# Where a decoder block's side work stands: the first operand sums on VectorE, and the weight combinations two at a time

## The reference

```
proj = rms_norm(x) @ w_in                      # pool, gate, conv a, conv b, gate, q, k, v, gate
y_pool = window means of u minus u, mapped per group, scaled
y_conv = silu(layer_norm(depthwise_conv31(a * sigmoid(b)) + bias)) @ conv_pw
y_attn = softmax(q k^T + alibi, window 128, sinks) @ v       # 8 query heads, 2 key heads
y      = concat(y_pool * silu(g1), y_conv * silu(g2), y_attn * silu(g3))
out    = rms_norm(x + y @ w_out) * final_g
```

## Time and profile before

| | |
|---|---|
| median of three runs | 1467.82 us (1467.74 to 1469.67) |
| profiled execution | 1469.99 us, its span 1468.3 us |
| busy | PE 97%, DVE 77%, ACT 34%, POOL 28% |
| attention stage | to about 660 us |
| output stage | from about 1140 us |

### The profile page before, as it was taken

One profiled execution on the slowest core, in us unless ns is written; L12 is line 12 of the kernel. 1 busy time (PEld: TensorE's weight loads), 2 busy tenths in 40 slices (PEclk: granted clock), 3 DMA queues, 4 the chain that ended last, 5 costly groups with the idle time before them and its releaser, 6 DMA issues.

```text
span 1468.3 us, 20261 instructions
## 1 busy us (share of the span) xinstructions
PE 1424.7 (97%) x6992; PEld 1154.8 (79%) x6992; DVE 1136.6 (77%) x2317; ACT 504.0 (34%) x1232; POOL 406.7 (28%) x627
## 2 busy tenths in 40 slices
PE   4999999999999999999999999999999799999997
PEld 4878787777878787878878778787787578888886
DVE  4574848576674738577999988989989978888886
ACT  5444444544444434341112111121112233333332
POOL 5323433332423232120011011010120245555552
PEclk9999999999999999999999999999999899999999
DMA  9116171615241130817033032130425655554531
GB/s 313 60 32 241 58 271 43 257 58 230 99 149 80 57 143 8 307 46 212 1 144 129 16 137 106 43 129 15 173 88 227 272 188 187 158 167 157 161 129 72
DMA packets 77804, 196.80 MB, mean 134 GB/s; under 512 B 14256, under 2 KB 41264, under 8 KB 70064
## 3 DMA queue, kind: packets, MB, share of 16 engines
q1 hardware_dynamic: 63184, 181.40, 32.8%
q10 hardware_dynamic: 14560, 14.68, 3.8%
HBM read 114.27 MB, written 81.79 MB: 134 GB/s over the span
## 4 chain that ended last, share of the span: by engine, by line
PE 80%; DVE 14%; ACT 4%; issue 1%; POOL 1%; DMA 0%; SPq 0%; POOLq 0%; DVEq 0%; ACTq 0%
PE wide L231 12%; PE wide L233 12%; PE wide L232 12%; PE pair L231 10%; PE pair L233 9%; PE pair L232 9%; DVE m_tail L1596 3%; ACT a_rows L672 2%; DVE a_pT L794 2%; DVE a_rows L770 2%; PE turn L233 2%; PE turn L231 2%; PE turn L232 2%; PE pair L1812 2%; PE pair L917 2%; PE wide L946 1%
## 5 line engine op out<-in xcount | busy, mean ns | idle before, releaser
L1596 DVE SCALAR_TENSOR_TENSOR m_tail<-m_tail,m_taps 128x512 f32<-128x512 f32 x480 | 344.4, 762 | 6.5
L231 PE MATMUL pair<-xT,w_hi 128*128 128x512 f32 x640 | 261.2, 408 | 8.2 <-DVE xT L224 4.5
L232 PE MATMUL pair<-xT,w_lo 128*128 128x512 f32 x640 | 251.0, 392 | 0.0
L233 PE MATMUL pair<-xT,w_hi 128*128 128x512 f32 x640 | 250.7, 392 | 0.0
L107 POOL TENSOR_TENSOR pool_carrier<-pool_carrier 128x1 f32<-128x1 f32 x83 | 26.5, 319 | 619.3 <-DVE m_meanvar L1605 402.7
L1395 POOL TENSOR_TENSOR operand_sums<-m_y 128x512 f32<-128x512 f32 x80 | 111.1, 1392 | 180.6 <-PE wide L233 129.1
L231 PEld LDWEIGHTS pair<-xT,w_hi 128*128 128x128 f32 x640 | 121.1, 189 | 33.6 <-DVE a_q L815 7.3
L233 PEld LDWEIGHTS pair<-xT,w_hi 128*128 128x128 f32 x640 | 120.7, 189 | 26.2
L232 PEld LDWEIGHTS pair<-xT,w_lo 128*128 128x128 f32 x640 | 121.2, 189 | 19.9
L231 PE MATMUL wide<-x_first,w_hi 128*128 128x512 f32 x320 | 126.8, 396 | 0.0
L231 PE MATMUL wide<-xT,w_hi 128*128 128x512 f32 x320 | 126.8, 396 | 0.0
(11 more groups left out here) (211 smaller groups left out, 2876.9 us busy)
## 6 DMA issues: line engine op xcount, KB each, us to landing
xT_scratch<-xT SPq DMA_DIRECT2D x16, 2048.0 KB, 15.0
xs<-in_x_dram SPq DMA_DIRECT2D x32, 512.0 KB, 5.2
x_first<-xT_scratch SPq DMA_DIRECT2D x16, 1024.0 KB, 7.4
xT<-xT_scratch SPq DMA_DIRECT2D x16, 1024.0 KB, 9.1
combo_scratch<-stage SPq DMA_DIRECT2D x28, 512.0 KB, 2.8
m_y<-y_scratch ACTq DMA_DIRECT2D x14, 1024.0 KB, 6.7
y_scratch<-y_out SPq DMA_DIRECT2D x8, 1024.0 KB, 5.7
y_scratch<-y_out SPq DMA_DIRECT2D x16, 512.0 KB, 3.1
```

The lines of the kernel that those rows point to most:

```text
L231: nc.tensor.matmul(out, w_hi, x_hi, start=first, stop=False)
L232: nc.tensor.matmul(out, w_lo, x_hi, start=False, stop=False)
L233: return nc.tensor.matmul(out, w_hi, x_lo, start=False, stop=last)
L1596: nc.vector.scalar_tensor_tensor(out=conv[:, i, :], in0=h[:, i, j:j + TB], scalar=taps[:, i, j:j + 1], in1=conv[:, i, :], op0=ALU.mult, op ...
```

## The change

The five sums of the first pair are formed by VectorE, at the head of the last mixer block. ScalarE makes the high parts between cb0 and cb1 instead of behind gp1. VectorE makes the low parts behind the layer norm statistics instead of behind `gate_conv`. In the attention stage the combination steps go as (0, 1), (2, 3), (4, 5), (6) behind q0, q1, q2 and q3, on ScalarE and on VectorE, and VectorE makes the low parts at the same place as the additions. `Combos` itself, its two stage buffers, and SP's order are as they were.

```diff
# ScalarE, attention stage
+        def combo(unit, steps):
             if unit is not None:
-                combos.split_hi(act, unit, i)
+                for i in steps:
+                    combos.split_hi(act, unit, i)
...
             q_hi(n, 0)
-            combo(unit, 0)
+            combo(unit, (0, 1))
...
             q_hi(n, 1)
-            combo(unit, 1)
+            combo(unit, (2, 3))
...
             if not final:
                 st.square(act, n + 1)
             q_hi(n, 2)
-            combo(unit, 2)
+            combo(unit, (4, 5))
...
             q_hi(n, 3)
-            combo(unit, 3)
+            combo(unit, (6,))
...
-                if j < 3:
-                    combo(unit, 4 + j)
# VectorE, attention stage
-        def combo(unit, step):
+        def combo(unit, steps):
             if unit is not None:
-                if step < STEPS:
-                    combos.add(dve, unit, step)
-                if step:
-                    combos.split_lo(dve, unit, step - 1)
+                for i in steps:
+                    combos.add(dve, unit, i)
+                for i in steps:
+                    combos.split_lo(dve, unit, i)
...
             make_q_lo(n, 0)
-            combo(unit, 0)
+            combo(unit, (0, 1))
             if not first:
                 output(n - 1, 3, (n, slot("o3")))
             for t in range(1, GROUP):
...
                 make_q_lo(n, t)
-                combo(unit, t)
+                combo(unit, range(2 * t, min(2 * t + 2, STEPS)))
...
-                combo(unit, 4 + j)
# GpSimd, mixer stage
-        for i in range(STEPS):
-            operand_add(0, 0, i)
# ScalarE, mixer stage
             for i in range(2):
                 from_proj(m, r, f"cb{i}", sig[:, i, :], ACT.Tanh, 0.5)
+                if final and i == 0:
+                    for step in range(STEPS):
+                        operand_hi_of(0, 0, step)
...
-            if final:
-                for i in range(STEPS):
-                    operand_hi_of(0, 0, i)
# VectorE, mixer stage
+        def first_operand_sums():
+            dve.wait_ge(y_loaded[0], 16)
+            dve.wait_ge(proj_full, PROJ * (NB - 1))
+            for i in range(STEPS):
+                if len(LEFT[i]) == 3:
+                    left, op, right = LEFT[i]
+                    nc.vector.tensor_tensor(operand_sums[:, i, 1], y_block(0, left), y_block(0, right), SIGN[op]).then_inc(first_sum, 1)
...
+            if final:
+                first_operand_sums()
             glu(m, r, 0)
...
                 layer_norm_stats(n - 1)
+                if final:
+                    for i in range(STEPS):
+                        operand_lo_of(0, 0, i)
                 some_taps(m, r, 0, LEAD)
...
-            if final:
-                for i in range(STEPS):
-                    operand_lo_of(0, 0, i)
```

More of the change, by code:

```diff
@@ L679, in gate_tanh @@
             nc.scalar.activation(tanh[:, t % 2, :], proj[p % 2][:], ACT.Tanh, scale=0.5).then_inc(tanh_done, 1)
-        def combo(unit, i):
+        def combo(unit, steps):
             if unit is not None:
-                combos.split_hi(act, unit, i)
+                for i in steps:
+                    combos.split_hi(act, unit, i)
         def body(n, unit=None):
@@ L1069, in mixer_output_programs @@
     y_loaded = [sem("y_loaded0"), sem("y_loaded1")]
-    operand_sum, operand_hi, operand_lo = sem("operand_sum"), sem("operand_hi"), sem("operand_lo")
+    first_sum, operand_sum, operand_hi, operand_lo = sem("first_sum"), sem("operand_sum"), sem("operand_hi"), sem("operand_lo")
     gain_loaded = sem("gain_loaded")
@@ L1390, in operand_add @@
                 pool.wait_ge(y_loaded[q], y_uses(n, q))
[L1391 to L1394, removed]
+                pool.wait_ge(acc_full, step_of(p - 1, i) + 1)
                 nc.gpsimd.tensor_tensor(operand_sums[:, i, 1], y_block(q, left), y_block(q, right), SIGN[op]).then_inc(operand_sum, 1)
@@ L1454, in operand_hi_of @@
             p = 2 * n + q
-            if len(LEFT[i]) == 3:
-                act.wait_ge(operand_sum, sum_of(p, i) + 1)
+            if len(LEFT[i]) == 3 and isinstance(p, int) and p == 0:
+                act.wait_ge(first_sum, sum_of(p, i) + 1)
+            elif len(LEFT[i]) == 3:
+                act.wait_ge(operand_sum, sum_of(p, i) + 1 - sum_of(0, STEPS))
             else:
```

## The result

| | before | after |
|---|---|---|
| median | 1467.78 us (4 runs) | 1502.04 us (4 runs, 1497.97 to 1502.19) |
| ratio, estimated over all runs | | 1.0225, 95% interval 1.0205 to 1.0245 |
| profiled execution, its span | 1469.99, 1468.3 | 1501.89, 1499.8 |

The change makes the kernel 34 us slower. 1497 was forecast, with a range of 1479 to 1508.

What follows compares the result with a forecast made beforehand. TensorE, busy 97% of the span, was taken to bound the kernel; 1468.3 - 6.7 (first-pair sums) + 35.7 (combination steps) = 1497.3 against its span, 1497 us against the median, range 1479 to 1508.

Steps and rivals of the forecast that it cites:

- The wait for the stores: Attention blocks with combinations: high part 2 waits for store 0, to 292.3, and step 3's sum for store 1, to 293.6.
- The gating as the first link: Attention stage: o3's copy comes 2.0 us later, so GpSimd's gating ends at 286.8 instead of 284.8, with combination stores queued behind.
- the fourth piece of traffic as the last: Store 1 lands fourth among 512 KB pieces, behind the gated block's two and store 0, at 293.6 (bounds 290.5 and 294.9).
- The stall before v: Four blocks with combinations: TensorE waits 8.1 us for q2's low part before v (bounds 5.0 and 9.4).
- The clock: TensorE's clock drops after each stall ahead of v, losing about 2.2 us more per block (bounds 1.5 and 3).
- The tiles' gain: Attention tiles: steps 4 to 6 leave them, gaining 1.37 us a block, 5.5 us over four (bounds 0 and 5.5).
- Part B: Attention stage, combination steps grouped behind q: stall plus clock less the tiles, +8.9 us a block, +35.7 us over four.
- Part A: Last mixer block, first pair's sums on VectorE: -6.7 us, from -4 to -8, off TensorE's 9.6 us output-stage wait.
- main term: Last mixer block: eleven lead taps fall from 13.32 to 8.62 us without GpSimd's five sums, 4.70 us gained (lower bound nothing).
- a third of the loss back, 0.9 us: Last sixteen taps start earlier and end before pair 1's third sum begins, regaining 0.9 of 2.72 us (bounds 0 and 2.7).
- I take half, 1.1 us: Output stage: with 4.0 us of waiting the clock may stay up; half of the 2.0 to 2.2 us loss counted saved.
- the stall reaches q2 as well: Rival: raw data over 1.3 us later makes o3's copy hold q2, some 2 us more a block, 1505 us; chance 0.08.

Runs made afterwards that it cites:

- stores_first: The changed kernel with SP issuing combination stores 0 and 1 ahead of the gated block's store; 1489.43 us, ratio 1.0139.
- b_only: The kernel before with only the attention-stage edits (combination steps two at a time behind q); 1506.76 us, ratio 1.0255.
- port_reads: The changed kernel with twelve GpSimd additions of 128x256, result unused, where GpSimd's five first-pair sums stood; 1507.02 us, one run.
- port_writes: The changed kernel with twelve GpSimd memsets of 128x256, result unused, where GpSimd's five first-pair sums stood; 1500.75 us, one run.
- busy: The changed kernel with 28 extra unused TensorE products ahead of v in the four blocks with combinations, written out instead of looped; 1498.68 us, ratio 1.0200.
- regrouped: The kernel before with the mixer-stage edits and steps 0-1 behind q0, 2-3 behind q2 after the squares, 4-5 behind q3, 6 in tile 0; 1463.48 us.
- both: As `regrouped`, with pair 1's three sums beside the last taps moved from GpSimd to VectorE behind those taps; 1463.01 us, ratio 0.9958.

## Why the prediction was right, and where a term was off

- **The wait for the stores.** From q0's high part to high part 2 I had 17.0 us (275.3 to 292.3), and it is 17.05 (293.37 to 310.42); to step 3's sum 18.3 and 18.36. The gating as the first link (o3 copied 1.9 us later; 2.0 forecast) and the fourth piece of traffic as the last were right in block 3. `stores_first` shows what the chain left out: without the gating, the stores land only behind the `xT` stores, so that link alone was worth 3.2 us of ScalarE's wait (7.98 to 4.80), where its expectation had 5.6.
- **The stall before v.** Forecast 8.1 us; 7.1, 7.9 and 8.4 in blocks 2 to 4. In block 1 it is 10.9. There the raw quarters come 1.3 us later (a wait of 2.2 instead of 0.8 us) and store 1 takes 7.8 us to land instead of 6.0. That is 3.1 of the 3.5 us by which this block is longer. It changes from execution to execution: with the same attention stage, block 1's stall is 10.6 us in `b_only`, 9.8 in `port_reads` and 7.9 in `port_writes`, where the wait for the raw quarters is 0.2 us. Why the transfers are slower in some was not tried.
- **The clock.** Forecast 2.2 us a stall, with 1.5 and 3 as bounds. `busy` gives 1.7 us: right in kind, a little large, inside the bounds.
- **The tiles' gain.** The whole difference of 1.37 us a block was counted as won, and most of it came. From v's first product to its end, block 3 takes 53.49 us after the change (319.93 to 373.42), 52.68 before (293.86 to 346.54), and block 5, without combinations, 51.50. `busy` tells the clock and the tiles apart: with the clock up it takes 51.75, so the tiles give 0.9 us and the clock takes 1.7.
- **Part B.** Forecast +35.7, measured 38.35 in the trace, and block 1's 3.5 us is more than the difference. In `port_writes`, whose block 1 is not longer, the four blocks take 356.94 us, +35.35. So the number came out by the mechanism; within a block the clock's part and the tiles' gain are both 0.5 us smaller than forecast, and offset each other.
- **Part A.** Forecast -6.7, measured -4.2 in the trace. Its main term, 4.70 us from the lead taps, came to 4.69 (13.32 to 8.63). The three small ones failed: "a third of the loss back, 0.9 us" was 0.0, since all three sums of pair 1 still ran beside the last taps (the taps ended 1.8 us after the third sum began, where I had them end before it). "I take half, 1.1 us" for the clock was 0: it fell 2.8 us into the 4.9 us wait. Staying up would have won nothing either, since the load of `y` sets when z comes: in `regrouped` the clock is back about a microsecond sooner, TensorE waits 1.6 us for z instead of 0.9, and z is turned 15.2 us behind the product that the first low part releases, all the same. And 0.5 us was given back there (14.7 us before the change, 15.2 after), which I had not looked at. The failed 0.9 could have been seen in the trace of the kernel before: starting 4.7 us earlier and with 1.8 us lost to two sums, the taps end at 1147.5, and the third sum begins at 1146.50:

```profile
1146.50 1.32 POOL L1395 TENSOR_TENSOR operand_sums<-m_y 128x512 f32<-128x512 f32 x1 [1.15 <-PE wide L233]
```

- **The rivals.** None of them came. The one nearest was "the stall reaches q2 as well": the raw quarters were late in block 1, by the 1.3 us of q2's cover, and TensorE shows no second long wait there.

## What to carry to other kernels

When side work is moved to where an engine is idle, ask first for the waits it brings with it and what is queued behind them: two high parts of 0.63 us became an 8 us stall, because they had to wait for the stores of a two-deep buffer and now stood ahead of four squares and a query tile. Count a store's landing from its place in the issue queue and behind all traffic under way, not from when its data is ready. When a wait is shortened, look for what else is due behind it: here a load issued by another engine took back all that `both` won. And a slow stretch of VectorE whose operations have two inputs in SBUF is worth reading beside GpSimd's timeline before anything is made of the loads.

## What the runs showed of the hardware that was not expected

- A GpSimd memset costs VectorE's taps nothing (8.63 us for eleven, with 3.6 us of memsets beside them); twelve additions of the same shape in their place cost them 3.93 us.
- A store of 512 KB issued 10 to 11 us behind two of 2 MB took 9 us to land (`stores_first`); the median of such stores in the kernel before is 2.8.
- The granted clock fell some 2.8 us into TensorE's wait at the output stage in the changed kernel and 4.0 us into it in the kernel before, and behind the wait it stayed down for 4.8 and 4.7 us. So a wait of 4.9 us was no cheaper in its after-effect than one of 9.6. It varies: in `regrouped`, with a wait of 4.9 us too, the clock fell only when TensorE was at work again and came back after 3.8 us. Windows of one microsecond, first in the wait of the changed kernel, then where it ends in `regrouped`:

```profile
1186.00:1187.00 1.00, 0.00 (x0) 1.00 1.07 433
1187.00:1188.00 1.00, 0.00 (x0) 0.80 1.01 401
1188.00:1189.00 1.00, 0.00 (x0) 0.50 1.07 453
```

```profile
1149.00:1150.00 1.00, 0.28 (x1) 0.30 (x2) 1.00 (x2) 0.00 (x0) 0.00 (x0) 1.00 0.81 322
1150.00:1151.00 1.00, 1.00 (x4) 0.77 (x3) 1.00 (x3) 0.00 (x0) 0.00 (x0) 0.57 1.26 366
```
